# Experts in groups of three, two and one: another order for the MoE stage of a streaming encoder step

## The reference

```python
logits = jnp.einsum('nd,de->ne', t, p['router_w']) + p['router_b']
vals, idx = lax.top_k(logits, TOP_K)                 # 4 of 32 experts
wts = jax.nn.softmax(vals, axis=-1).reshape(-1)
...
hh = t[toks] @ p['w_up'][e] + p['b_up'][e]           # 1024 -> 2048
glu = jnp.minimum(hh[:, :D_FF], SWIGLU_LIMIT)
lin = jnp.clip(hh[:, D_FF:], -SWIGLU_LIMIT, SWIGLU_LIMIT)
y = (glu * jax.nn.sigmoid(SWIGLU_ALPHA * glu) * (lin + 1.0)) @ p['w_down'][e] + p['b_down'][e]
out = jax.ops.segment_sum(y * w, row_tok, num_segments=n_tok)
```

## Time and profile before

| what | value |
|---|---|
| median of three runs | 2036.42 us |
| profiled execution | 2040.91 us, span 2039.1 us |
| expert stage, first to last matmul | 834.27 to 1952.24 us |
| TensorE busy | 1763.6 us (86%) |
| weights of the 32 experts | 384 MB, nearly all in this stage |

### The profile page before, as it was taken

The page is one execution under the profiler, slowest core; times in us unless marked ns, Lnnn a source line. Parts: engine busy times, 40 slices in busy tenths (PEclk is TensorE's granted clock), DMA queues, the critical chain, the costliest instruction groups (busy, mean ns, idle before and its releaser), DMA issues. The chain is left out here.

```text
span 2039.1 us, 51682 instructions
## 1 busy us (share of the span) xinstructions
PE 1763.6 (86%) x20847; PEld 1043.7 (51%) x20848; DVE 747.8 (37%) x2280; ACT 361.2 (18%) x726; POOL 206.9 (10%) x277
## 2 busy tenths in 40 slices
PE   4999989788998893899899898998998989877847
PEld 1546468366655543456465455554554545433423
DVE  2422335326333357433333333332333333222315
ACT  0001211432121101122122121121121121111100
POOL 0000010110000220011011010010100100000025
PEclk9998966879899895899999999999999999988869
DMA  9543030910420627868978998989989899899763
GB/s 354 188 138 124 0 112 6 285 33 1 172 77 5 163 93 277 344 266 344 417 290 345 417 370 346 417 319 417 375 358 416 327 416 416 328 414 416 306 223 138
DMA packets 160309, 532.75 MB, mean 261 GB/s; under 512 B 24282, under 2 KB 65438, under 8 KB 127412
## 3 DMA queue, kind: packets, MB, share of 16 engines
q1 hardware_dynamic: 133760, 494.21, 62.1%
q0 software_dynamic: 7392, 22.81, 3.1%
q10 hardware_dynamic: 19028, 13.77, 2.2%
HBM read 496.62 MB, written 33.99 MB: 260 GB/s over the span
## 5 line engine op out<-in xcount | busy, mean ns | idle before, releaser
L1773 PE MATMUL psum<-arena 128*32 128x192 f32 (+1 forms) x11904 | 691.8, 391 | 87.2 <-issue 48.5
L1773 PEld LDWEIGHTS psum<-arena 128*32 128x32 f32 x11904 | 395.5, 113 | 381.4 <-issue 106.9
L1781 PE MATMUL psum<-arena 128*32 128x256 f32 x5952 | 348.8, 385 | 30.2 <-DMA arena<-in_w_down 30.2
L1832 DVE STREAM_TRANSPOSE arena<-psum 128x320 f32<-128x320 f32 (+1 forms) x186 | 83.7, 450 | 629.1 <-PE psum L1773 629.1
L1781 PEld LDWEIGHTS psum<-arena 128*32 128x32 f32 x5952 | 182.8, 111 | 167.7 <-DMA arena<-in_w_down 34.4
L1757 ACT ACT_TABLE_LOAD x93 | 119.3, 1283 | 255.8 <-issue 222.7
L1757 ACT ACTIVATE arena<-arena 128x160 f32<-128x160 f32 (+1 forms) x186 | 57.6, 310 | 452.4 <-DVE arena L1837 452.4
L414 PE MATMUL psum<-arena 128*128 128x512 f32 (+2 forms) x400 | 129.0, 481 | 0.0
L1735 POOL COPY arena<-arena 128x1 uint32 (+1 forms) x94 | 17.1, 181 | 967.7 <-DVE arena L1826 930.1
L414 PEld LDWEIGHTS psum<-arena 128*128 128x128 f32 x400 | 70.9, 210 | 58.1 <-issue 58.1
L1738 POOL DMA_INDIRECT arena<-d_u,arena x94 | 92.1, 979 | 74.0 <-POOL arena L1735 74.0
(11 more groups left out here) (382 smaller groups left out, 1565.0 us busy)
## 6 DMA issues: line engine op xcount, KB each, us to landing
arena<-in_w_up SPq DMA_DIRECT2D x128, 2048.0 KB, 12.2
arena<-in_w_down SPq DMA_DIRECT2D x64, 2048.0 KB, 27.4
arena<-in_w_ada SPq DMA_DIRECT2D x10, 2048.0 KB, 15.9
d_y<-arena ACTq DMA_DIRECT2D x372, 32.0 KB, 5.7
arena<-in_w_in SPq DMA_DIRECT2D x5, 2048.0 KB, 7.7
d_y<-arena SPq DMA_DIRECT2D x1, 10240.0 KB, 33.1
arena<-in_cache_ckv SPq DMA_DIRECT2D x8, 1024.0 KB, 5.7
arena<-in_x_prompt SPq DMA_DIRECT2D x2, 2048.0 KB, 21.4
```

Source lines behind the costliest of these rows:

```text
L1773: ins = pe.matmul(S[h][c * U:(c + 1) * U, 0:2 * U * (b1 - b0)].rearrange("p (g b j) -> p g b j", g=2, j=U), xT[:, 2 * q + k, :], up[par][q ...
L1781: ins = pe.matmul(Y[c * U:(c + 1) * U, 0:256], hidT[:, n, :], down[par][n // 4][:, n % 4, c * 256:(c + 1) * 256], start=(n == 0), stop=(n ...
L1832: dve.transpose(wide, S[h][:, 0:2 * U * w]).then_inc(s["h_turned"], 1)
```

## The change

The eight groups of one long and three short experts become eleven groups of three sizes: four of one long and three short, two of one long and two short, and five pairs. Eleven experts (`LONG_RANK`, by rank) have buffer 0 and stay while others pass through buffer 1 (`SHORT_RANK`). A long expert is cut into as many parts as its group has shorts. TensorE, VectorE and SyncE have a loop for each size, one after another, with a pass for each group; there are 42 runs of units. In the router stage the cut into parts takes its factors from two new rows of the constant table.

```diff
-GROUPS, LONG_MIN = 8, 3
-MIN_UNITS = GROUPS * LONG_MIN + NE - GROUPS
-MAX_UNITS = TOK * TOPK // U + NE + GROUPS * (LONG_MIN - 1)
-SEGS = 6
+RUN_SIZES = ((3, 4), (2, 2), (1, 5))
+RUNS = [(k, ng, sum(n for _, n in RUN_SIZES[:i]), sum(k0 * n for k0, n in RUN_SIZES[:i]))
+        for i, (k, ng) in enumerate(RUN_SIZES)]
+MIN_UNITS = 2 * NS
+MAX_UNITS = TOK * TOPK // U + NE + NS - NL
...
-RANK_AT = [list(range(1, 9)), [0] + list(range(15, 8, -1)), list(range(23, 15, -1)), list(range(31, 23, -1))]
+LONG_RANK = [4, 2, 1, 3, 5, 6, 12, 7, 10, 11, 26]
+SHORT_RANK = [0, 21, 30, 17, 28, 29, 16, 31, 23, 19, 27, 22, 14, 25, 15, 24, 8, 13, 20, 9, 18]
...
+    for k, ng, g0, _ in RUNS:
+        c[:, C_LEAST + g0:C_LEAST + g0 + ng] = k
+        for i in range(k):
+            part[0, i, g0:g0 + ng] = -(-512 // k)
+            part[1, i, g0:g0 + ng] = -(-512 // k) * (k - 1 - i)
...
-            with sp.Fori(0, GROUPS - 1) as j:
-                within(j)
-                switch(j + (GROUPS + 1), 1, cum(sp, j * SEGS + 5, least=1))
-                switch(j + 1, 0, cum(sp, j * SEGS + 6, least=1))
-            within(GROUPS - 1)
+            for k, ng, g0, m0 in RUNS:
+                whole = ng if g0 + ng < NL else ng - 1
+                if whole:
+                    with sp.Fori(0, whole) as j:
+                        for i in range(1, k + 1):
+                            next_short(j * k + (m0 + i))
+                        switch(j + (g0 + 1), 0, cum(sp, j * (2 * k) + 2 * (m0 + k), least=1))
...
-            with pe.Fori(0, GROUPS) as j:
-                hi = cum(pe, j * SEGS)
-                for g in range(SEGS):
-                    lo, hi = hi, cum(pe, j * SEGS + (g + 1))
+            for k, ng, g0, m0 in RUNS:
+                with pe.Fori(0, ng) as j:
+                    hi = cum(pe, j * (2 * k) + 2 * m0)
+                    for g in range(2 * k):
+                        lo, hi = hi, cum(pe, j * (2 * k) + (2 * m0 + g + 1))
```

More of the change, by code:

```diff
@@ L55 @@
 C_RANK = C_TOK + NT
-NCONST = C_RANK + NE
+C_LEAST = C_RANK + NE
+C_PART = C_LEAST + NE
+NCONST = C_PART + 2 * KMAX * NL
+assert NCONST <= BIAS_AT
 R_SEL4, R_RESET, R_SELC = 0, MH * P, MH * P + TOK
@@ L80, in const_tables @@
         c[:, C_TOK + t] = t * P + p
-    c[:, C_RANK:C_RANK + NE] = np.array(RANK_AT).reshape(-1)
+    c[:, C_RANK:C_RANK + NE] = LONG_RANK + SHORT_RANK
+    c[:, C_LEAST:C_LEAST + NE] = 1
+    part = np.zeros((2, KMAX, NL), np.float32)
+    for k, ng, g0, _ in RUNS:
[3 more added lines that the diff above has]
+            part[1, i, g0:g0 + ng] = -(-512 // k) * (k - 1 - i)
+    c[:, C_PART:C_PART + 2 * KMAX * NL] = part.reshape(-1)
     r = np.zeros((1 + DEC_B, NROWS), np.float32)
@@ L1328, in stage_output_router @@
     key, need, rank, per, pack, pack_e, add_e = (v.cut(26808 + NE * i, NE) for i in range(7))
[L1329 to L1332, removed]
+    pack2 = v.cut(27032, NL)
+    part_of, part_of_i = v.cut(27044, KMAX, NL), v.cut(27078, KMAX, NL).bitcast(U32)
+    seg, seg_end, seg_at = (v.cut(27112 + 2 * NS * i, NS, 2) for i in range(3))
+    part_i, part = v.cut(27240, 5, NE).bitcast(U32), v.cut(27400, 5, NE)
+    assert KMAX * NL <= 33 and 6 * NS <= 126
     over = v.cut(21208, NT, NE)
@@ L1592, in _ @@
             dve.tensor_copy(v.order[0:1, :], rank[0:1, :]).then_inc(s["order_ready"], 1)
[L1594 to L1597, removed]
-            link(ins)
[L1599 to L1605, removed]
+            mul, off = (v.const[:, C_PART + m * KMAX * NL:C_PART + (m + 1) * KMAX * NL
+                                ].rearrange("p (i g) -> p i g", i=KMAX) for m in range(2))
+            link(dve.tensor_tensor(part_of, per[:, 0:NL].unsqueeze(1).to_broadcast([P, KMAX, NL]), mul, ALU.mult))
+            link(dve.tensor_tensor(part_of, part_of, off, ALU.add))
+            link(dve.tensor_copy(part_of_i, part_of))
+            link(dve.tensor_scalar(part_of_i, part_of_i, 9, None, ALU.logical_shift_right))
+            dve.tensor_copy(seg[:, :, 0], per[:, NL:])
+            link(dve.tensor_copy(part_of, part_of_i))
+            run = lambda a, k, ng, m0: a[:, m0:m0 + k * ng].rearrange("p (g i) two -> p i g two", i=k)
+            for k, ng, g0, m0 in RUNS:
+                ins = dve.tensor_copy(run(seg, k, ng, m0)[:, :, :, 1], part_of[:, 0:k, g0:g0 + ng])
+            link(ins)
+            flat = lambda a: a.rearrange("p m two -> p (m two)")
+            link(dve.tensor_tensor_scan(flat(seg_end), v.ones[:, 0:2 * NS], flat(seg), 0.0, ALU.mult, ALU.add))
             link(dve.tensor_tensor(seg_at, seg_end, seg, ALU.subtract))
@@ L1609, in _ @@
             dve.tensor_copy(v.cum[0:1, 1:], flat(seg_end)[0:1, :])
[L1611 to L1614, removed]
+            dve.memset(pack2, 0.0)
+            dve.tensor_scalar(pack[:, NL:], seg_at[:, :, 0], 127.0 * (P + P * P), None, ALU.add)
+            link(dve.tensor_scalar(pack[:, 0:NL], part_of[:, 0], float(P + P * P), None, ALU.mult))
+            link(dve.scalar_tensor_tensor(pack[:, 0:NL], part_of[:, 1], float(P * P), pack[:, 0:NL],
                                           ALU.mult, ALU.add))
-            link(dve.scalar_tensor_tensor(pack[:, 0:GROUPS], third[:, 1], float(P * P), pack[:, 0:GROUPS],
-                                          ALU.mult, ALU.add))
-            link(dve.scalar_tensor_tensor(pack2, seg[:, :, 4], float(P), seg[:, :, 2], ALU.mult, ALU.add))
+            for k, ng, g0, m0 in RUNS:
+                own = slice(g0, g0 + ng)
+                ins = dve.tensor_tensor(pack[:, own], pack[:, own], run(seg_at, k, ng, m0)[:, 0, :, 1], ALU.add)
+                if k == 3:
+                    ins = dve.scalar_tensor_tensor(pack2[:, own], run(seg, k, ng, m0)[:, 2, :, 0], float(P),
+                                                   run(seg, k, ng, m0)[:, 1, :, 0], ALU.mult, ALU.add)
+                if k == 2:
+                    ins = dve.tensor_copy(pack2[:, own], run(seg, k, ng, m0)[:, 1, :, 0])
+            link(ins)
             link(dve.tensor_tensor(prod, pick.rearrange("p a e -> p e a"),
@@ L1717, in _ @@
                 load_down(long0, 0, h)
-            with sp.Fori(0, GROUPS - 1) as j:
-                within(j)
-                switch(j + (GROUPS + 1), 1, cum(sp, j * SEGS + 5, least=1))
-                switch(j + 1, 0, cum(sp, j * SEGS + 6, least=1))
-            within(GROUPS - 1)
-            done = cum(sp, GROUPS * SEGS - 1, least=1)
+            for k, ng, g0, m0 in RUNS:
+                whole = ng if g0 + ng < NL else ng - 1
[4 more added lines that the diff above has]
+                        switch(j + (g0 + 1), 0, cum(sp, j * (2 * k) + 2 * (m0 + k), least=1))
+                if whole < ng:
+                    for i in range(1, k):
+                        next_short(whole * k + m0 + i)
+            done = cum(sp, 2 * NS - 1, least=1)
             sp.wait_ge(s["down_done"], done * 2 + 1)
@@ L1742, in _ @@
             gather(0)
-            total = cum(pool, GROUPS * SEGS, least=MIN_UNITS)
+            total = cum(pool, 2 * NS, least=MIN_UNITS)
             with pool.Fori(0, total) as b:
@@ L1752, in _ @@
             act.sem_inc(s["y_out"], 1)
-            total = cum(act, GROUPS * SEGS, least=MIN_UNITS)
+            total = cum(act, 2 * NS, least=MIN_UNITS)
             with act.Fori(0, total) as b:
@@ L1812, in _ @@
             pe.sem_inc(s["down_done"], 1)
-            with pe.Fori(0, GROUPS) as j:
-                hi = cum(pe, j * SEGS)
-                for g in range(SEGS):
-                    lo, hi = hi, cum(pe, j * SEGS + (g + 1))
[L1817 to L1821, removed]
+            for k, ng, g0, m0 in RUNS:
+                with pe.Fori(0, ng) as j:
+                    hi = cum(pe, j * (2 * k) + 2 * m0)
+                    for g in range(2 * k):
+                        lo, hi = hi, cum(pe, j * (2 * k) + (2 * m0 + g + 1))
+                        with pe.Fori(lo, hi) as b:
+                            if g % 2 == 0:
+                                unit(b, j * k + (m0 + g // 2 + 1), 1)
+                            else:
+                                unit(b, j + (g0 + 1), 0)
         @block.vector
@@ L1849, in _ @@
             x_turn()
[L1850 to L1867, removed]
+            for k, ng, g0, m0 in RUNS:
+                with dve.Fori(0, ng) as j:
+                    hi = cum(dve, j * (2 * k) + 2 * m0)
+                    for g in range(2 * k):
+                        lo, hi = hi, cum(dve, j * (2 * k) + (2 * m0 + g + 1))
+                        at = j * k + (NL + m0 + g // 2) if g % 2 == 0 else j + g0
+                        e = dve.value_load(v.order[0:1, bass.ds(at, 1)], min_val=0, max_val=NE - 1)
+                        dve.tensor_copy(bias.rearrange("p g (m k) -> p k g m", k=4),
+                                        biasT[:, :, bass.ds(e, 1), :].rearrange("p k e (g m) -> p k (e g) m", g=2)
+                                        ).then_inc(s["bias_sel"], 1)
+                        with dve.Fori(lo, hi) as b:
```

(8 more changed lines are left out.)

23 lines of the change are left out of this document (12 added, 11 removed).

## The result

The changed kernel takes 1984.32 us (median of 4 runs, 1983.85 to 1985.31), the kernel before beside it 2037.44 us (2035.61 to 2042.65): a ratio of 0.9736 [0.9717, 0.9755]. The prediction was 1982.2. The execution that was profiled took 1985.31 us, 55.6 less than the profiled one of before; the sum had said 54.2.

What follows compares the result with a forecast made beforehand. It held the expert stage bound by neither TensorE nor the weight queue alone, losing time to fill, turns and weight waits. Stage -55.1 and VectorE +0.9 us gave -54.2, so 2036.4 became 1982.2 us, stated range 1974 to 2004.

Steps and rivals of the forecast that it cites:

- the sum: Whole kernel: -55.1 us for the expert stage and +0.9 us for VectorE make -54.2 us.
- Turns: TensorE's outer-loop jumps, expert stage: three in triples, one in doubles, 8.9 us each, 35.6 us together; pairs free.
- Rival 1: Expert stage: pairs pay their turns too, so TensorE ends last, 5.4 us later, 1987.6 us; chance 0.28.
- rival 2: Expert stage: doubles' turn is free too, the queue takes most back, 2.4 us stay, 1979.8 us; chance 0.12.
- Waits for weights up to the last short of the doubles: Triples and doubles, expert stage: TensorE waits 19.7 us in all, mainly 5.0 and 12.3 at two longs.
- The fill: Start of the expert stage: the first unit takes 13.4 us, 3.0 too many.
- The piece of weights: Weight queue, expert stage: a 2 MB load takes 5.5 us, 33.0 an expert, plus 2.3 us latency.
- the rule: Weight queue: the n-th load of a chain begun at b lands at b + 33.0 n + 2.3; stage ends at 1897.2.
- Rival 3: Weight queue: loads are slower without rest for 330 us, 5.74 us per 2 MB, giving 2008.5 us; chance 0.09.
- Rival 4: Expert stage: memory path can't hold 408 GB/s; at 357 it takes 31 us more, 2068 us; chance 0.04.
- VectorE's chain: Integer arithmetic ahead of the expert stage, which TensorE waits for: +0.9 us, between 0.3 and 2.
- What follows the stage: Everything after the expert stage's end stays as it is: 0 us difference.

Runs made afterwards that it cites:

- fold: Changed kernel with TensorE's doubles and triples passing through one body of two runs in an inner loop; 1977.41 us, 0.9693 of the kernel before.
- fold_before: Kernel before, with TensorE's eight groups each made three passes through a body of two runs; ranks, groups and loads unchanged; 2030.66 us, ratio 0.9954.
- fold_mixed: fold_late with the eleven groups' sizes in another order and a table of ranks to match; 1960.64 us, 0.9619 of the kernel before.
- changed_again: The changed kernel as it is, timed once more beside three later runs; 1983.27 us, 0.9736 of the kernel before.
- plain_ranks: Changed kernel with another table: longs are ranks 1 to 11 in order, shorts rank 0, then 31 down to 12; 2007.28 us, 0.9849 of before.
- pair_delay: Changed kernel with 160 extra unused matmuls at the head of each of the five pair passes; 2002.39 us, 0.9813 of the kernel before.
- fold_late: fold with each pass's third run bound read between its two runs, not at the head; 1965.91 us, 0.9642 of the kernel before.
- fewer_bytes: Changed kernel with reloads bringing half of each down piece, 10 MB of 12 an expert, outputs wrong; 1938.51 us, 0.9503 of the kernel before.

## Why the prediction was right, point by point

**Turns: right in kind, the price too low.** The doubles pay and the pairs nearly don't, as the forecast had it: 1.0 us a turn in place of nothing, and as much at the entries of two loops, put at below 0.5. Rival 1 (eight paying turns) and rival 2 (three) fall by the timeline. The triples' turns cost 9.6, 9.9 and 9.0 us in place of 8.9, the doubles' about 13 (7.1 of standing, and 13.1 from its first to its last up matmul, 6.0 more than 7.1). Most of the doubles' 6.0 is the second stand of 2.3 us and 3.1 for the low clock, which lasts to 1512.4. Why TensorE stands twice in a turn over four units and once in one over six isn't settled. The prediction held for rival 1 that the seven turns of before cost the same "whatever the queue did"; but the queue moved 407 to 420 GB/s in all seven, so they don't show that.

The packets show that such a turn reads its code again. Counted in units of TensorE's code, before reads 6 + 7 x 6 = 48, after 12 + 3 x 6 + 4 = 34, fold 6 and fold_before (27 packets by its page) 2. From before to after, from after to fold and from before to fold_before that is 14, 28 and 46 units fewer for 25, 52 and 83 packets: 1.8 a unit each time, 29 to 30 KB at 16.4 KB a packet. (fold_mixed, with ten units more than fold, has 16 packets more, 1.6 a unit.) With pairs that read again, four turns of two units more, after would have shown about 99 packets, not 85. So a jump back over 3.6 packets, some 59 KB, was kept and one over 7.2, some 118 KB, was not. By the Trainium skill's page "Runtime: NRT & Kernel Launch", section "Instruction fetch mechanics", the two-block window would have made the first pay and the 128 KiB would have spared the second; these runs agree with neither.

**Waits for weights up to the last short of the doubles: right at the two longs, at the shorts only in the sum.** The second triple's long waited 4.9 (5.0 predicted), the doubles' first long 12.0 (12.3). The shorts' 3.1 in all (2.4) lie elsewhere than foretold: 1.8 was put at the short behind the doubles' first long, which lost 0.2; a short of the first triple lost 1.4 in place of 0.3, and the doubles' first short 1.5, of which 1.0 is the entry of the loop and no wait for weights. The fill took 1.6 too many in place of 3.0. That is luck of the execution: the granted clock came back 3.0 us into the first unit where it had taken 5.8 in before, and in changed_again the fill was 2.8. With the turns' 6 more, that short ended at 1572.5 in place of 1568.6.

**The piece of weights: the term that was mis-sized.** "(101.5 - 2.3) / 18 = 5.5 us a piece" was carried over to ten experts, so 10 x 33.0 + 2.3 = 332.3 us. They took 323.4, from 1567.1 to 1890.5, that is 8.9 less, or 5.35 a piece with 2.3 for latency.

The 5.5 was read from chains that did not start where it put their start. SyncE's timeline of before has an expert issued 31 and 29 us ahead of the two chains of the earlier trace rows, and the table by stretches has the queue at its full rate where they begin:

```profile
1342.88 2.31 SPq L1693 DMA_DIRECT2D arena<-in_w_up  x4
...
1763.18 2.31 SPq L1693 DMA_DIRECT2D arena<-in_w_up  x4
```

```profile
1370.00:1380.00 10.00, 8.74 (x169) 5.25 (x164) 4.18 (x14) 1.90 (x3) 1.00 (x2) 1.00 1.03 415
1790.00:1800.00 10.00, 7.32 (x124) 4.21 (x120) 4.17 (x14) 0.62 (x2) 1.16 (x2) 0.84 1.03 419
```

So the three experts stood behind the end of a load. Counted from the issue that found the queue at rest, the four chains of before are four experts each and took 131.1 to 132.8 us, 132.2 in the mean. Against them the ten experts have 36 pieces more and took 191.2 us more: 5.31 a piece, which leaves 4.8 us once for a chain that starts from rest. Laid through all runs again as an estimate, 5.31 and 4.8 end the stage of before at 1951.0 (1952.2 measured) and, with the turns as measured, that of after at 1894.0 (1893.4); 5.35 and 2.3 would end before 16 us too early. So the rule had spread a cost paid once for each chain over its pieces. What makes up the 4.8 isn't shown. Rival 3 rests on the same reading: from 1763.18 the experts down at 1863.53 are three, and 100.4 less 4.8 is again 5.31 a piece. Rival 4, a memory path that can't hold the rate, falls by the 409 GB/s over 328 us.

So the stage ended at 1893.4 where 1897.2 was forecast: 3.9 late at the end of the doubles, 8.9 won on the queue, and the last half of the down matmuls 2.9 in place of 1.7. Two errors of opposite sign, the turns too cheap and the pieces too dear, made the sum look better than its terms were.

**VectorE's chain: right.** VectorE's first step and its first product, against the earlier trace rows:

```profile
800.99 0.17 DVE L1612 TENSOR_TENSOR arena<-arena 128x33 f32<-128x33 f32 x1
...
804.11 1.89 DVE L1643 TENSOR_TENSOR arena<-arena 128x1024 f32<-128x1024 f32 x1
```

From one to the other it is 3.12 us in place of 2.59; TensorE stands 23.71 us ahead of the one-hot matmuls, where the chain ends, in place of 23.00: 0.7 more (0.9 predicted). That the stage still started 0.7 earlier comes from the stages ahead, which the change doesn't touch, and a first gather 0.6 faster.

**What follows the stage: missed.** "What follows its end stays as it is" was wrong by 3.2 us, of which 2.4 is the wait at the barrier. The final loads of the combine stage are queued behind the last weights, as SyncE's timeline shows:

```profile
1853.33 12.12 SPq L1722 DMA_DIRECT2D arena<-in_w_down  x2
1871.66 5.27 SPq L1754 DMA_DIRECT2D arena<-d_x  x1
```

The wait was 15.5 to 18.4 us in all kernels but plain_ranks, whose last long has three units, so that these loads are done well before the end, and there it was 11.7. The traces put the difference on the last store of the experts: from its issue to its landing it took 8.2 us in after, 5.7 in before and 1.5 in plain_ranks, and from its landing to the combine stage's first matmul it is 8.2 us in all three. That the loads slow this store is argued from these runs; it was not tried apart. The other 0.8 of the 3.2 us isn't explained.

**Where the gain came from.** Long turns fewer by three (seven of 64 us in all before, four of 41.6 now) and half of the waits for weights; the stage's mean of 386 GB/s says how far it is from a queue that never rests. The queue decides in the last stretch: pair_delay put 45 us of work on TensorE there and the total rose by 17, and with fewer bytes the total fell by 47. Ahead of it TensorE's turns come through in part: in the traces fold's turns and passes up to the last short of the doubles cost some 8 us less than the changed kernel's, that short ends 5.0 us earlier, and the stage is 5.7 shorter.

## What to carry to other kernels

Read a kernel with two weight buffers as a queue: for each load, compare the work that covers it (here 10.4 us a unit and 8.7 of slack) with its 32 us, and pair experts so that the cover is never short; the rule laid through the trace of before foretold an end 4 us off in 1060, although two of its terms were off by more than that. Count the code between a loop's turns: written-out runs that jump back far read their code again, 9 to 13 us a turn here, while a nest with two units of code stood 1.2 to 2.0 us a pass. Take a rate from the longest chain there is, look in the timeline whether the queue was at rest when it began, and keep what a chain costs once apart from the price of a piece.

## What the runs showed that was not expected

- One bound read at the head of a nested loop's pass costs much: 2.0 us a pass with three reads, 1.2 with the third moved behind the first run; the total fell by about 9 us from fold to fold_late.
- One queue of 2 MB loads kept 409 GB/s for 328 us, with 417 in a hundred of them; the rate did not fall off over that stretch.
- The unit behind a long turn is slow because the granted clock is at 0.50 for its first 3.7 to 8.5 us; a turn of the pairs, with 1.0 us of standing, leaves the clock at 1.00.
- Whether a long turn would be cheaper with the queue at rest, no run shows: the queue moved 406 to 420 GB/s while TensorE stood in the long turns of before and after, and 413 to 424 in those of fewer_bytes.
